# Feed-forward of a hybrid decoder block: weight sums on one engine, half units of the down projection among the products

## The reference

```python
h = rms_norm(x, norm_ffn_pre[l])
gate = causal_dwconv(jnp.einsum("btd,df->btf", h, ffn_w_gate[l]), ffn_conv_w[l], ffn_conv_b[l])
up = jnp.einsum("btd,df->btf", h, ffn_w_up[l])
ffn_out = jnp.einsum("btf,fd->btd", jax.nn.gelu(gate, approximate=True) * up, ffn_w_down[l])
x = x + rms_norm(ffn_out, norm_ffn_post[l])
```

## Time and profile before

| | |
|---|---|
| runs | 2922.47, 2929.03, 2929.09 us |
| the profiled execution | 2925.74 us, its span 2924.1 us |
| granted TensorE clock, mean | 0.990 |
| busy: PE, DVE, ScalarE, POOL | 97%, 57%, 38%, 24% |
| DMA | 361.00 MB, mean 123 GB/s |

### The profile page before, as it was taken

The page is one execution under the profiler, slowest core; times in us unless marked ns, Lnnn a source line. Parts: engine busy times, 40 slices in busy tenths (PEclk is TensorE's granted clock), DMA queues, the critical chain, the costliest instruction groups (busy, mean ns, idle before and its releaser), DMA issues.

```text
span 2924.1 us, 41716 instructions
## 1 busy us (share of the span) xinstructions
PE 2834.1 (97%) x16287; PEld 2495.5 (85%) x16287; DVE 1677.9 (57%) x1508; ACT 1108.2 (38%) x1287; POOL 711.0 (24%) x438
## 2 busy tenths in 40 slices
PE   7999999999999999999869999999999999999997
PEld 6888888888888888888769989899998989899896
DVE  4332344344332233432578769696786969688697
ACT  3243443332222222222344444444444444444443
POOL 1000001000000000000143445444353544435353
PEclk9999999999999999999989999999999999999999
DMA  4234233332233334334514364636456473655645
GB/s 182 87 86 114 87 94 105 104 98 96 87 90 90 93 101 158 129 130 172 173 58 137 123 156 105 155 119 138 137 116 157 103 162 109 136 140 119 158 102 230
DMA packets 426496, 361.00 MB, mean 123 GB/s; under 512 B 10462, under 2 KB 354658, under 8 KB 423280
## 3 DMA queue, kind: packets, MB, share of 16 engines
q1 hardware_dynamic: 395552, 291.53, 32.7%
q0 software_dynamic: 26192, 58.91, 10.2%
q10 hardware_dynamic: 4608, 8.39, 0.7%
HBM read 300.06 MB, written 58.72 MB: 123 GB/s over the span
## 4 chain that ended last, share of the span: by engine, by line
PE 73%; DVE 18%; issue 6%; ACT 1%; POOL 1%; DVEq 0%; DMA 0%; ACTq 0%; SPq 0%; POOLq 0%
PE ps L512 18%; DVE op_ring L1902 9%; PE ps L515 9%; PE ps L812 7%; PE ps L737 6%; PE ps L829 5%; PE ps L831 5%; PE ps L830 5%; PE ps L816 4%; PE ps L536 3%; PE ps L537 3%; PE ps L538 3%; DVE arena L1959 2%; DVE arena L1962 2%; DVE arena L1541 1%
## 5 line engine op out<-in xcount | busy, mean ns | idle before, releaser
L1520 DVE TENSOR_TENSOR w_lo<-raw,w_hi 128x2048 fp32r<-128x2048 f32 x124 | 284.3, 2292 | 563.2 <-ACT w_hi L933 563.2
L1425 POOL TENSOR_TENSOR arena<-quad_ring 128x1024 f32<-128x1024 f32 x176 | 486.5, 2783 | 368.1 <-DVE op_ring L1902 315.5
L1902 DVE TENSOR_TENSOR op_ring<-quad_ring,op_ring 128x1024 fp32r<-128x1024 f32 x170 | 333.6, 1967 | 232.4 <-ACT op_ring L1170 232.4
L1902 DVE TENSOR_TENSOR op_ring<-arena,op_ring 128x1024 fp32r<-128x1024 f32 x220 | 384.6, 1748 | 44.6 <-ACT op_ring L1170 44.2
L812 PE MATMUL ps<-hl,op_ring 128*128 128x256 f32 x2816 | 367.7, 283 | 0.4 <-issue 0.4
L812 PEld LDWEIGHTS ps<-hl,op_ring 128*128 128x128 f32 x2816 | 351.1, 192 | 3.0 <-issue 2.6
L933 ACT CAST w_hi<-raw 128x2048 fp32r<-128x2048 f32 x124 | 236.4, 1907 | 260.9 <-PE ps L538 205.1
L1170 ACT CAST op_ring<-arena 128x1024 fp32r<-128x1024 f32 x220 | 230.8, 1049 | 247.2 <-PE ps L816 125.7
L812 PE MATMUL ps<-h,op_ring 128*128 128x256 f32 x2112 | 277.2, 284 | 6.0 <-DVE h L1894 6.0
L512 PE MATMUL ps<-h_hi,w_hi 128*128 128x512 f32 x1152 | 281.3, 397 | 1.1 <-ACT w_hi L933 1.1
L512 PE MATMUL ps<-h_lo,w_hi 128*128 128x512 f32 x1152 | 272.9, 389 | 0.0
(11 more groups left out here) (288 smaller groups left out, 3787.3 us busy)
## 6 DMA issues: line engine op xcount, KB each, us to landing
raw<-in_w_in SPq DMA_DIRECT2D x88, 1024.0 KB, 5.2
quad_ring<-in_ffn_w_gate SPq DMA_DIRECT2D x88, 512.0 KB, 4.6
quad_ring<-in_ffn_w_up SPq DMA_DIRECT2D x88, 512.0 KB, 4.5
quad_ring<-in_ffn_w_down SPq DMA_DIRECT2D x88, 512.0 KB, 5.3
down_sums<-arena POOLq DMA_DIRECT2D x160, 256.0 KB, 6.2
raw<-in_w_out SPq DMA_DIRECT2D x20, 1024.0 KB, 5.0
merge_gates<-arena ACTq DMA_DIRECT2D x32, 256.0 KB, 2.0
raw<-in_w_up_a SPq DMA_DIRECT2D x8, 1024.0 KB, 5.6
```

What stands on the lines that cost most here:

```text
L1425: pool.tensor_tensor(dst, quads[(4 * p + a) % QRING], quads[(4 * p + b) % QRING], ALU.subtract if q == M7 else ALU.add).then_inc(ff_sum, 1)
L1520: dve.tensor_tensor(w_lo[:, s, :], raw[:, s, :], f32(w_hi[:, s, :]), ALU.subtract).then_inc(lo_ready, 1)
L1902: dve.tensor_tensor(op_lo[(o + 1) % 3], source(o), f32(op_hi[(o + 1) % 3]), ALU.subtract).then_inc(ff_lo, 1)
```

## The change

What it does:

1. **Products.** hi and lo of h stand side by side, so the hi weights take one matmul of 512 columns for each of eight row tiles (`times_h`): the result has two halves of 256 columns in one bank, hi weights by hi of h and by lo of h. The lo weights add to the first half as before. DVE adds the two halves at the end (`both_halves`), and its combinations are 512 columns wide.
2. **Weight sums.** All five sums of a pair are made on DVE, each into the sum buffer of the op's own slot. There are four operand slots (`slot_of`) in place of three, and POOL sums nothing. The quarters have one buffer each, the down weights two. In each interval DVE makes the sum of op k + 3 and the lo part of op k + 2, ScalarE the hi part of op k + 3.
3. **Half units.** A half unit stands in the order among the products: after M2 and after M6 of each pair (`woven`). It belongs to the group of two hidden tiles before. Each half unit starts its banks anew and is copied out and added to DRAM by itself. For this ScalarE has three staging buffers, `STAGE = (0, 1, 2, 0)` for the four banks, each free when the DMA from it has landed (`acc_added`). The first step has four half units, the steps 1 to 9 eight each, the last one eight among its products and four at the end, the last four by token halves (`tail`).
4. **Transition.** The differences and sums of the normalised rows that POOL made are made by DVE.

The core of the diff:

```diff
+def woven(p):
+    d = D0 + 2 * (p % 2)
+    return [(p, q) for q in (M1, M4, M3, M2, d, M5, M7, M6, d + 1)]
+FIRST = [(0, q) for q in (M4, M2, M3, M5, M1, M7, M6)] + [(1, q) for q in PRODUCTS] + woven(2) + woven(3)
+MIDDLE = woven(0) + woven(1) + woven(2) + woven(3)
+FINAL = (woven(0) + woven(1) + [(2, q) for q in (M1, D0, M4, M3, D0 + 1, M2, M5, D0 + 2, M7, M6, D0 + 3)]
+         + [(3, q) for q in PRODUCTS] + [(4, D0 + d) for d in range(4)])
...
+        stage = arena[:, a0:a0 + 3 * T].rearrange("p (s t) -> p s t", s=3)
+        STAGE = (0, 1, 2, 0)
...
+            def load_pair(i, p):
+                pair = PAIRS * i + p
+                before = (i, p - 1) if p else (i - 1, 3)
+                sp.wait_ge(ff_sum, 5 * pair - 1)
+                sp.wait_ge(ff_lo, done(*before, M4))
+                load_quad(i, p, A22)
+                load_quad(i, p, A12)
+                sp.wait_ge(ff_sum, 5 * pair)
+                sp.wait_ge(ff_lo, done(*before, M3))
+                load_quad(i, p, A11)
+                load_quad(i, p, A21)
...
-                for r in range(2):
-                    for j in range(HALF):
-                        pe.matmul(ps[:, bank, 0:TH], w[0][:, j, :], h[:, j, r, :],
-                                  start=(r == 0 and j == 0 and q not in (M7, M6)), stop=False, skip_group_check=True)
+                for j in range(HALF):
+                    pe.matmul(ps[:, bank, :], w[0][:, j, :], h[:, j, :, :].rearrange("p r t -> p (r t)"),
+                              start=(j == 0 and q not in (M7, M6)), stop=False, skip_group_check=True)
                 pe.wait_ge(ff_lo, o + 1)
                 for j in range(HALF):
                     mm = pe.matmul(ps[:, bank, 0:TH], w[1][:, j, :], h[:, j, 0, :], start=False, stop=(j == HALF - 1),
                                    skip_group_check=True)
...
+            def down(i, p, q, pos):
...
+                pe.wait_ge(ff_hi, o + 1)
+                pe.wait_ge(ff_lo, o + 1)
+                pe.wait_ge(act_lo_ready, 2 * group + 2)
+                for n in range(TT):
+                    tok = slice(n * P, n * P + P)
+                    past(pe, dn_evac, 4 * n_down + n - 3)
+                    for j in range(2):
+                        pe.matmul(ps[:, n, :], act_hi[:, f + j, tok], w[0][:, j, :], start=(j == 0), stop=False)
+                        pe.matmul(ps[:, n, :], act_hi[:, f + j, tok], w[1][:, j, :], start=False, stop=False)
+                        mm = pe.matmul(ps[:, n, :], act_lo[:, f + j, tok], w[0][:, j, :], start=False, stop=(j == 1))
+                    mm.then_inc(dn_done if n < TT - 1 else ff_op, 1)
...
+            def down_copy(i, p, q, n):
+                n_down, s = down_of(i, p, q), STAGE[n]
...
+                past(act, acc_added[s], 16 * (n_down if s else 2 * n_down + n // 3))
+                act.copy(stage[:, s, :], ps[:, n, :]).then_inc(dn_evac, 1)
+            def interval(i, k):
+                ops = sequence(i)
+                p, q = ops[k - 1] if k else (None, None)
+                if k and q >= D0:
+                    down_copy(i, p, q, 3)
+                if k + 3 < len(ops) or sequence(i) is not FINAL:
+                    hi(i, k + 3)
+                if k < len(ops) and ops[k][1] >= D0 and ops[k][0] < 4:
+                    for n in range(3):
+                        down_copy(i, *ops[k], n)
+                if q in (M1, M4, M3):
+                    keep_product(i, p, q, {M1: 6 + p % 2, M4: 4, M3: 5}[q])
+                if q in (M7, M6):
+                    if p % 2 == 0:
+                        first_tap(i, p, 0 if q == M7 else 1)
+                    else:
+                        hidden_hi(i, p, 0 if q == M7 else 1)
+                for n in range(2):
+                    if k > 2 + n and ops[k - 2 - n] in ((0, M6), (2, M6)):
+                        gelu(i, ops[k - 2 - n][0], n)
...
+            for n_down in range(4 * (GROUPS - 1)):
+                for n in range(TT):
+                    d, s = n_down % 4, STAGE[n]
+                    pool.wait_ge(dn_evac, 4 * n_down + n + 1)
...
+                        pool.dma_start(dst, src, accum_op=ALU.add).then_inc(acc_added[s], 16)
...
+            def weight_sum(i, pos):
...
+                dve.tensor_tensor(op_sum[slot_of(i, pos)], quads[:, a, :], quads[:, b, :],
+                                  ALU.subtract if q in (M7, M6) else ALU.add).then_inc(ff_sum, 1)
+            def after_m5(i, p, bank):
+                plus_m5(i, p, bank)
+                both_halves(i, p, 0, 1, 3)
+                m1_minus_m5(i, p, bank)
+            def interval(i, k):
+                ops = sequence(i)
+                if sequence(i) is not FINAL or k + 3 < len(ops):
+                    weight_sum(i, k + 3)
+                if sequence(i) is not FINAL or k + 2 < len(ops):
+                    lo(i, k + 2)
+                p, q = ops[k - 1] if k else (None, None)
+                up = k > 0 and p % 2 == 1
+                if q == M2:
+                    after_m2(i, p, 7 - p % 2)
+                elif q == M5:
+                    after_m5(i, p, 6 + p % 2)
+                elif q == M7:
+                    after_m7(i, p)
+                    if up:
+                        times_gate(i, p, 0)
...
```

More of the change, by code:

```diff
@@ new lines, in ff_step, with need @@
+            def ff_step(i, start=0, end=None):
+                for pos, (p, q) in list(enumerate(sequence(i)))[start:end]:
+                    if q >= D0:
+                        down(i, p, q, pos)
+                    else:
+                        product(i, p, q, pos)
+            def need(count):
+                pe.wait_ge(th_lo, count)
+            need(2)
+            times_h(0, 0, M4, 4)
+            need(4)
+            times_h(0, 1, M2, 6)
+            for r in range(4, 8):
+                turn_pieces(r)
@@ L823, in down_half, with tail @@
+            ff_step(0, len(SLOT_FIRST))
+            with pe.Fori(1, LAST) as i:
+                ff_step(i)
+            ff_step(LAST, 0, PRODUCTS_END)
+            def tail(d, tiles, parts, before):
+                w = [t[d].rearrange("p (j n) -> p j n", j=2) for t in (op_hi, op_lo)]
+                b0 = 0 if d % 2 == 0 else 4
                 for n in tiles:
@@ new lines, in _ @@
+            pe.wait_ge(dn_evac, 16 * (GROUPS - 1))
+            for part in range(2):
+                pe.wait_ge(act_lo_ready, 2 * GROUPS - 1 + part)
+                for d in range(2):
+                    if part == 0:
+                        pe.wait_ge(ff_lo, ops_before(LAST) + PRODUCTS_END + d + 1)
+                    if d == 1:
+                        pe.wait_ge(ff_part, 6 * 2 * GROUPS)
+                    tail(d, HALVES[0], (part,), nothing)
+            for e in range(2, 8):
+                half, d = divmod(e, 4)
+                if half == 0:
+                    pe.wait_ge(ff_lo, ops_before(LAST) + PRODUCTS_END + d + 1)
+                tail(d, HALVES[half], (0, 1), lambda n: pe.wait_ge(down_evac, 2 * (e - 2) + n % 2 + 1))
@@ L1170, in hi @@
[L1170 to L1182 removed]
+                    part = A22 if q == M4 else A11
@@ new lines, in hi, with keep_product @@
+                    quad_loaded(act, i, p, part)
+                    src = quads[:, part, :]
+                else:
+                    act.wait_ge(ff_sum, summed(i, p, q))
+                    src = op_sum[slot]
+                act.copy(op_hi[slot], src).then_inc(ff_hi, 1)
+            def keep_product(i, p, q, bank):
+                pair, which = PAIRS * i + p, {M1: X1, M4: X4, M3: X3}[q]
+                act.wait_ge(ff_op, done(i, p, q))
+                if isinstance(i, int) and (i, p) == (0, 0):
@@ new lines, in plus_m2, with m1_minus_m2 @@
+            def plus_m2(i, p, bank):
+                pair, first = PAIRS * i + p, isinstance(i, int) and (i, p) == (0, 0)
+                dve.wait_ge(ff_copy, 3 * pair + (1 if first else 2))
+                dve.wait_ge(ff_op, done(i, p, M2))
+                dve.tensor_tensor(ff_x[:, X4, :], ff_x[:, X4, :], ps[:, bank, :], ALU.add).then_inc(ff_part, 1)
+            def m1_minus_m2(i, p, bank):
+                pair = PAIRS * i + p
+                dve.wait_ge(ff_half, 4 * pair + 1)
+                dve.tensor_tensor(ff_x[:, X4, :], ff_x[:, X1, :], ps[:, bank, :], ALU.subtract).then_inc(ff_part, 1)
@@ new lines, in plus_m5, with m1_minus_m5 @@
+            def plus_m5(i, p, bank):
+                pair, first = PAIRS * i + p, isinstance(i, int) and (i, p) == (0, 0)
+                dve.wait_ge(ff_copy, 3 * pair + (2 if first else 3))
+                dve.wait_ge(ff_op, done(i, p, M5))
+                dve.tensor_tensor(ff_x[:, X3, :], ff_x[:, X3, :], ps[:, bank, :], ALU.add).then_inc(ff_part, 1)
+            def m1_minus_m5(i, p, bank):
+                dve.wait_ge(ff_part, 6 * (PAIRS * i + p) + 3)
+                dve.tensor_tensor(ff_x[:, X1, :], ff_x[:, X1, :], ps[:, bank, :], ALU.subtract).then_inc(ff_part, 1)
@@ L2037, in _ @@
             lo(0, 3)
```

(4 more changed lines are left out.)

724 lines of the change are left out of this document (288 added, 436 removed).

## The result

The changed kernel took 2942.68 us in the median of 4 runs (2941.15 to 2945.31), the kernel before 2925.75 beside it: ratio 1.0059, interval 1.0041 to 1.0077, 17 us slower. The direction was forecast and the range held; the size, 45 us, was not: it is 17 to 28. That the direction came true was luck, as the stages show.

What follows compares the result with a forecast made beforehand. TensorE bounds the kernel, DVE next; after the change a staging buffer's reuse sets 40 pairs at 32.8 us. With 134.3 us besides, 1446.3 against 1398.0, less 3.5: 44.8 us slower, 2971 us; 8-in-10 range 2888 to 3020.

Steps and rivals of the forecast that it cites:

- Part 1: Products with hi and lo side by side: 2.77 us each for 2.88, 33 us over 308 products.
- If PE still sets the pace: Condition on the products' 33 us saving: that PE, at 30.3 us a pair, remains what binds.
- Part 2: Weight sums on DVE: 3.4 us subtractions return to 1.14; DVE about 24 us of a pair's 30.3.
- Part 3: Half units: bank 3's copy waits for bank 0's DMA; pair 32.8 us, step 131 us, 3.4 more than before.
- Links: ScalarE and DVE queue work from bank 3's copy to the next half unit's copy 0: 8.5 (up pair 8.9), 9.5 us.
- L1: A pair's first half unit, copy 0's start to its staging buffer's release: 7.7 us, with a landing of 6.8.
- L2: A pair's second half unit, copy 0's start to its staging buffer's release: 6.9 us, with a landing of 6.0.
- c: Time of a pair with half units, forecast 32.8 us; the sum turns from faster to slower at 31.7.
- pair 1: First step's pair without half units: 22.4 us, of which 3 us charged for DVE binding.
- Part 4: Transition's row sums moved to DVE: pair 1 begins 3.5 us earlier; bounds 10 earlier, 5 later.
- Part 5: Last step: its last two pairs 71.4 us, including 9.5 of wait, and the tail 40.5 us (35 to 46).
- The rival on PE's side: PE sets the pace in the pairs after all, at 30.3 us: 55 us faster, 2871 us; chance 0.23.
- DMA traffic: Rival: DMA engines 0.75 busy, landings like the 7.6 or weight loads late; c = 34.4, 3034 us; chance 0.10.

Runs made afterwards that it cites:

- the POOL experiment: Two unread 128x1024 sums on POOL added in every half unit from the second group on, against the kernel with four staging slots: 3106.03 us, 1.0629.
- late copy: Changed kernel with bank 3's copy put behind the hi half of the operand three places on in ScalarE's queue: 2895.35 us, 0.9922.
- fourth slot: Changed kernel with a fourth staging buffer, its space gained by computing M7 with M6's moving operand (values not the reference's): 2885.04 us, 0.9890.
- longer turn: Changed kernel with POOL sending the sums of tiles 1 and 0 in the other order: 3143.21 us, 1.0762.
- e11: Four row sums of the transition back on POOL, against the kernel with bank 3's copy behind the hi half and the gain row early: 2889.39 us, 0.9887.

## Why the prediction came out as it did

- **Part 1**: right, 2.79 us a product for 2.77. "If PE still sets the pace" was the condition, and it held in part only.
- **Part 2**: right in its lengths (1.22 us throughout). The forecast said nothing of what it is worth, and no run shows it: the POOL experiment prices a sum on POOL, 2.7 us of DVE each.
- **Part 3**, the mechanism and its place: right, and shown three ways: late copy, fourth slot, longer turn. Links of 8.5, 8.9 and 9.5 us were forecast; by the means of both kinds of pair they are 8.4, 8.9 and 9.4. L1 was 7.7 and is 7.9.
- **The step that failed is the term "L2 has no load ahead: 6.0, and L2 = 6.9".** The landing is 4.8 us and L2 5.76, 1.1 less; with 40 pairs that is 45 us, more than the whole error of 25. The 6.0 came from a DMA issued between two weight loads, though the step itself said that L2 has none ahead. The trace before had the row that fits: eight first DMAs of a group between 1700 and 2700 us have no load within 5 us ahead, and they land in 4.4 to 6.0 us, 5.2 on the mean. One is issued at 2138.07:

```profile
down_sums<-arena POOLq DMA_DIRECT2D x1, 256.0 KB, 5.3
```

With 5.2 there c is 32.0 and the sum 11 us slower, 2937 us. With the measured 4.8 c is 31.6, the point where my own sum turned, and the forecast would have been no change.
- **The direction** came true by luck: the steps lose nothing, and the slowdown that was measured is the start, pair 1, the last two pairs and the tail, each longer than its term. The chain is still why the change gains nothing: with the late copy the same parts give a pair of 30.4 us.
- **Part 4**: wrong in sign by 6.3 us, within its bounds. The row operations did go from 4.50 to 2.35 us, and DVE was 5 us ahead at 1484 us, but of the sums taken over, most do not stand where DVE waited: from 1495 to 1514 us it has one gap, of 2.0 us, and the last lo of h ends 4.2 us later than before. The e11 run shows that POOL would be no cheaper.
- **Part 5**: the two last pairs are 76.4 for 71.4. PE's waits in them add up to 9.6 us, 3.0 of them just before the tail, about what was charged. The sum had put nothing for the clock. After three of the waits, of 1.9 to 2.3 us each, the granted clock fell to 1.2 GHz for a while, and matmuls of 512 columns started 0.43 us apart for 0.23; the mean over the two pairs is 0.93, about 5 us (PE's timeline, then the window with columns as in the earlier trace rows):

```profile
2824.03 0.47 PE L881 MATMUL ps<-op,act_hi 128*128 128x512 f32 x1 [2.06 <-DVE act_lo L1957]
...
2826.21 0.63 PE L882 MATMUL ps<-op,act_hi 128*128 128x512 f32 x1
2826.64 0.63 PE L883 MATMUL ps<-op,act_lo 128*128 128x512 f32 x1
...
2819.05:2895.40 76.35, 66.84 (x321) 55.92 (x319) 48.99 (x58) 35.62 (x52) 17.31 (x20) 0.93 0.72 137
```

The tail is 48.3 for 40.5: I let the rows "land during it", but SP's order puts the gain row behind two down loads that wait for DVE, and four reloads. I had added 4 us; the gain row alone was worth 6.
- **The rival on PE's side** (0.23) needed landings under 5.2 us on the mean of both turns; they are 6.9 and 4.8. DMA traffic (0.10): the share was 0.80, for 0.75 estimated, but L2's landing fell below that of before.

## What to carry to other kernels

Where a wait for a DMA stands in an engine's queue, first ask what stands behind it: moving one copy behind one conversion was worth 40 to 54 us and needed no space. A chain of landings and queue links can be summed link by link from rows of the kernel before, but take each landing from a DMA that has the same traffic just ahead of it; with 40 turns, 1 us in one term is the whole result. A change that saves work on the binding engine and adds a reuse of a buffer should be judged by both sums side by side, here 30.4 and 31.7. And a forecast whose direction comes true should be checked stage by stage before it is believed.

## What I had not expected of the hardware

- Accumulating into DRAM cost a DMA of 256 KB 3.3 us of landing in the median (6.4 for 3.1), 1.5 and 2.1 us for the first of a group (6.9 and 4.8 for 5.4 and 2.7), and its queue 2.7 times the engines' time (47.5% for 17.6%).
- POOL's issue of a plain DMA takes 0.54 us and of an accumulating one 0.86 (141.0 us for 263 and 218.5 for 253, by the windows).
- A sum on POOL cost DVE 2.7 us, also beside operations of 512 columns (2.8 and 2.2 us for 0.69 and 0.75): DVE's operation ended its own length behind POOL's.

By the Trainium skill, SBUF — State Buffer (Who interferes with whom), DVE with two SBUF inputs and GpSimd reading SBUF exclude each other: the trace with the added sums agrees (means of 2.2 to 2.8 us beside them for 0.69 to 1.22). Its fit of a GpSimd DMA, in DMA: Bandwidth & Descriptors (Anatomy of one DMA), gives an estimate of 2.6 us for these 256 KB. The shortest plain copies agree with it, the median is 3.1 us, and behind other transfers they take longer (the view of POOL's line, all 263 in the window):

```profile
DMA to landing us min/median/max: 2.6/3.1/7.5
```

The accumulating ones took 4.1 to 10.4 us in the changed kernel; of them the fit says nothing apart. The measurement decides.
